# Attention outputs on one Trainium2 core: the probabilities as the stationary operand, the value tile as the moving one

## The reference

```python
def _branch_attention(q, k_cat, v_cat, slopes, window, dilation):
    ...
    m = jnp.max(sc, axis=-1, keepdims=True)
    p = jnp.exp(sc - m)
    den = jnp.sum(p, axis=-1, keepdims=True)
    o = jnp.einsum("bnrhqk,bnkrhe->bnqrhe", p / den, v_cat.astype(jnp.float32))
```

## Time and profile before

| | |
|---|---|
| median of 3 runs | 2321.32 us |
| lowest and highest run | 2320.58 and 2321.41 us |
| span of the profiled execution, first to last instruction | 2320.7 us |
| TensorE busy, of the span | 2254.3 us |
| attention in that execution | about 1086.5 to 1592 us |

### The profile page before, as it was taken

How to read it: one execution, slowest core, us unless ns; L and a number is a source line. 1 busy time by engine, 2 the same in 40 slices (tenths; PEclk the granted TensorE clock), 3 DMA queues, 4 the chain that set the end, 5 groups by cost and what they waited for, 6 DMA issues and landing times.

```text
span 2320.7 us, 32020 instructions
## 1 busy us (share of the span) xinstructions
PE 2254.3 (97%) x10792; PEld 1886.7 (81%) x10792; DVE 1509.0 (65%) x2236; ACT 940.1 (41%) x1712; POOL 477.8 (21%) x415
## 2 busy tenths in 40 slices
PE   7999997999999999999999999999799999999997
PEld 6888786888888888877888888888688888888886
DVE  5333347766666667697666666675876666666778
ACT  4111135322223234464655655565533323223443
POOL 1000014423332201053000000001543333310113
PEclk9999998999999999999999999999899999999999
DMA  5111122333333377736333323343233333337764
GB/s 146 46 55 45 51 94 64 96 99 108 104 108 106 108 263 249 252 108 173 75 69 77 77 69 73 73 114 114 73 95 104 110 105 109 101 111 260 249 224 168
DMA packets 244853, 273.98 MB, mean 118 GB/s; under 512 B 18400, under 2 KB 157664, under 8 KB 242656
## 3 DMA queue, kind: packets, MB, share of 16 engines
q1 hardware_dynamic: 241504, 260.64, 37.0%
q10 hardware_dynamic: 3200, 11.54, 1.5%
HBM read 198.20 MB, written 48.76 MB: 106 GB/s over the span
## 4 chain that ended last, share of the span: by engine, by line
PE 90%; DVE 4%; issue 2%; POOL 1%; ACT 1%; DMA 1%; DVEq 0%; SPq 0%; POOLq 0%; ACTq 0%
PE banks L1089 36%; PE banks L1136 15%; PE banks L883 11%; PE banks L1181 9%; PE banks L1012 7%; PE banks L1218 3%; PE banks L1233 3%; PE banks L1247 3%; PE banks L1261 1%; PE banks L931 1%; PE banks L1337 1%; DVE down_split L2212 1%; POOL xb_low L2731 1%; DMA raw_second<-in_o_w 0%; DVE x_lo L1933 0%
## 5 line engine op out<-in xcount | busy, mean ns | idle before, releaser
L1089 PE MATMUL banks<-xb_mid,up_split 128*128 128x512 f32 x2112 | 499.8, 392 | 4.7 <-DVE t_tile L1981 4.7
L1089 PEld LDWEIGHTS banks<-xb_mid,up_split 128*128 128x128 f32 x2112 | 400.5, 190 | 89.0 <-issue 5.5
L1136 PE MATMUL banks<-down_split 128*128 128x512 f32 x1848 | 423.0, 390 | 5.0 <-DVE down_split L2212 4.1
L1136 PEld LDWEIGHTS banks<-down_split 128*128 128x128 f32 x1848 | 345.6, 188 | 80.7 <-DVE down_split L2212 9.2
L1089 PE MATMUL banks<-xb_low,up_split 128*128 128x512 f32 x1584 | 373.5, 389 | 0.0
L1089 PEld LDWEIGHTS banks<-xb_low,up_split 128*128 128x128 f32 x1584 | 297.2, 188 | 62.2 <-issue 0.6
L2212 DVE TENSOR_TENSOR down_split<-down_raw,down_split 128x1024 fp32r<-128x1024 f32 x154 | 198.1, 1286 | 99.8 <-ACT down_split L1644 99.5
L1644 ACT CAST down_split<-down_raw 128x1024 fp32r<-128x1024 f32 x154 | 162.1, 1053 | 208.4 <-PE banks L1136 170.2
L2055 DVE TENSOR_TENSOR up_split<-sums,up_split 128x512 fp32r<-128x512 f32 x176 | 157.7, 897 | 130.0 <-ACT up_split L1499 129.7
L883 PE MATMUL banks<-x_hi,w_first 128*128 128x512 f32 x768 | 184.5, 392 | 1.2 <-ACT x_hi L1418 1.1
L2805 POOL TENSOR_TENSOR sums<-raw_up 128x512 f32<-128x512 f32 x88 | 119.6, 1361 | 320.3 <-DVE up_split L2055 162.2
(11 more groups left out here) (180 smaller groups left out, 3312.0 us busy)
## 6 DMA issues: line engine op xcount, KB each, us to landing
raw_up<-in_ffn_in_w SPq DMA_DIRECT2D x88, 512.0 KB, 5.1
down_raw<-in_ffn_out_w SPq DMA_DIRECT2D x154, 256.0 KB, 3.4
down_raw<-hid_spill SPq DMA_DIRECT2D x154, 256.0 KB, 4.0
hid_spill<-hid_mix SPq DMA_DIRECT2D x110, 256.0 KB, 2.4
down_second<-in_ffn_out_w SPq DMA_DIRECT2D x66, 256.0 KB, 3.2
k_stack<-k_parts SPq DMA_DIRECT2D x32, 512.0 KB, 6.2
raw_first<-in_conv_in_w SPq DMA_DIRECT2D x24, 512.0 KB, 3.7
hid_spill<-hid SPq DMA_DIRECT2D x44, 256.0 KB, 2.4
```

The source lines that it names most:

```text
L1089: mm = pe.matmul(bank(b_out), up_split[:, p, a, q * P:(q + 1) * P], block(RIGHT_OF[p], b)[:, q, :], start=(i == 0), stop=(i == len(passes) ...
L1136: mm = pe.matmul(bank(b_out), side[:, a, 0, i * P:(i + 1) * P], side[:, b, 1, :], start=(p in (M3, M5, M1, M2) and first and j == 0), stop ...
```

## The change

The operands of the output matmul change places. The transposed probabilities are now stationary, high part and low part in turn, and the value tile moves, 128 columns. A key tile takes two matmuls of 128 columns with a stationary operand each, all added up in one bank: 128 queries by 128 columns (64 features by the high values, 64 by the low values). The result is already queries by features. `o_second`, `o_sum`, `fold` and `turn_part` go. ScalarE scales columns 64 to 127 into `resid` (`scaled`), one pipeline step after the outputs, and VectorE then scales columns 0 to 63 and adds them to it there (`halves_added`). `o_done`, now VectorE's, frees the bank `OUT`; `o_scaled` is ScalarE's new signal. ScalarE's wait for `spilled` stands ahead of the first steps.

```diff
 # TensorE
-                    pe.wait_ge(*sum_done.at("attn", steps + s))
+                    pe.wait_ge(*o_done.at("attn", steps + s))
                     for j in range(i + 1):
-
-                        mm = pe.matmul(psum[:, OUT, 0:2 * P].rearrange("p (n q) -> p n q", n=2),
-                                       att["v_split"][pair % 2][:, j, e, :],
-                                       att["pt"][:, s % 2, :, j * P:(j + 1) * P],
-                                       start=(j == 0), stop=(j == i))
+                        for n in range(2):
+                            mm = pe.matmul(psum[:, OUT, 0:P], att["pt"][:, s % 2, n, j * P:(j + 1) * P],
+                                           att["v_split"][pair % 2][:, j, e, :],
+                                           start=(j == 0 and n == 0), stop=(j == i and n == 1))
                     mm.then_inc(pv_done.sem, 1)
-
-                def turn_part(s):
-
-                    pe.wait_ge(*sum_done.at("attn", steps + (s + 1)))
-
-                    pe.wait_ge(*o_done.at("attn", steps + s))
-                    if last and s + 1 in range(LEADS - HT, LEADS):
-                        pe.wait_ge(*lead_lo.at("attn", s + 2))
-
-                    pe.matmul(psum[:, TURN, 0:HD], att["o_sum"][:], att["fold"][:], start=True, stop=True) \
-                        .then_inc(o_turned.sem, 1)
...
                     scores(s + 1)
-                    if s >= 2:
-                        turn_part(s - 2)
                     turn_probs(s)
 # ScalarE
-                def second_part(s):
+                def scaled(s):
 
                     act.wait_ge(*pv_done.at("attn", steps + (s + 1)))
-
-                    act.wait_ge(*sum_done.at("attn", steps + s))
-                    act.copy(att["o_second"][:], psum[:, OUT, P:2 * P]).then_inc(second_done.sem, 1)
-
-                def divide(s):
-
-                    act.wait_ge(*o_turned.at("attn", steps + (s + 1)))
                     act.wait_ge(*rden_done.at("attn", steps + (s + 1)))
                     over, e, i = place(s, last)
                     pair = fixed + over
                     act.activation(resid[:, i, bass.ds(moving * P + (pair * P + e * HD), HD)],
-                                   psum[:, TURN, 0:HD], ACT.Copy, scale=rden[:, s % 2:s % 2 + 1]) \
-                        .then_inc(o_done.sem, 1)
+                                   psum[:, OUT, HD:P], ACT.Copy, scale=rden[:, s % 2:s % 2 + 1]) \
+                        .then_inc(o_scaled.sem, 1)
...
-                    if s >= 2:
-                        divide(s - 2)
                     probs_high(s)
                     if s >= 1:
-                        second_part(s - 1)
+                        scaled(s - 1)
                     exponentials(steps, s + 1)
...
+            act.wait_ge(spilled, 16)
             attend((0, 0), 0, 2, STEPS)
-            act.wait_ge(spilled, 16)
 # VectorE
-                def sum_parts(s):
-
-                    dve.wait_ge(*second_done.at("attn", steps + (s + 1)))
-
-                    dve.wait_ge(*o_turned.at("attn", steps + s))
-                    dve.tensor_tensor(att["o_sum"][:], psum[:, OUT, 0:P], att["o_second"][:],
-                                      ALU.add).then_inc(sum_done.sem, 1)
+                def halves_added(s):
+
+                    dve.wait_ge(*o_scaled.at("attn", steps + (s + 1)))
+                    over, e, i = place(s, last)
+                    pair = fixed + over
+                    o_tile = resid[:, i, bass.ds(moving * P + (pair * P + e * HD), HD)]
+                    dve.scalar_tensor_tensor(out=o_tile, in0=psum[:, OUT, 0:HD],
+                                             scalar=rden[:, s % 2:s % 2 + 1], in1=o_tile,
+                                             op0=ALU.mult, op1=ALU.add).then_inc(o_done.sem, 1)
...
                     probs_low(s)
                     if s >= 1:
-                        sum_parts(s - 1)
+                        halves_added(s - 1)
                     invert(s)
 # GpSimd
-            pool.wait_ge(*xn_ready.at("norm2", HT))
-            pool.tensor_tensor(att["fold"][:], ident[:, 0:HD], ident[:, HD:P], ALU.add) \
-                .then_inc(dist_ready.sem, 1)
```

More of the change, by code:

```diff
@@ L258, in trunk @@
                "neg_log": at(204, "neg_log", [SEQ]), "bias": at(208, "bias", [SEQ]),
-               "dist": at(212, "dist", [SEQ], F16), "v_t": at(214, "v_t", [HALF]),
-               "o_second": at(216, "o_second", [P]), "o_sum": at(216.5, "o_sum", [P]),
-               "fold": at(217, "fold", [HD])}
+               "dist": at(212, "dist", [SEQ], F16), "v_t": at(214, "v_t", [HALF])}
         dist_i = at(8, "dist_i", [SEQ], I32)
@@ L371, in trunk @@
         ph_done = signal("ph_done", attn=STEPS * PAIRS)
-        second_done = signal("second_done", attn=STEPS * PAIRS)
-        o_done = signal("o_done", attn=STEPS * PAIRS)
+        o_scaled = signal("o_scaled", attn=STEPS * PAIRS)
         lo_ready = signal("lo_ready", **chunks)
@@ L414, in trunk @@
         pl_done = signal("pl_done", attn=STEPS * PAIRS)
-        sum_done = signal("sum_done", attn=STEPS * PAIRS)
+        o_done = signal("o_done", attn=STEPS * PAIRS)
         rden_done = signal("rden_done", attn=STEPS * PAIRS)
@@ L419, in trunk @@
         gain_step = signal("gain_step", norm2=4)
-        dist_ready = signal("dist_ready", attn=2)
+        dist_ready = signal("dist_ready", attn=1)
         c12_sum = signal("c12_sum", **of_down(HT))
@@ L871, in _ @@
             grant(pe, lead_turned, half_done, chunk_done, tok_done, down_done, down_tile, up_done, xt_turned, v_turned, s_done, p_turned,
-                  pv_done, o_turned)
+                  pv_done)
             def weights(n, ph, moving=0):
@@ L1375, in _ @@
                   xn_first, xr_done, t3_hi_done,
-                  tc_hi_done, lead_hi, k_hi_done, q_hi_done, v_done, vv_hi, exp_done, ph_done, second_done,
-                  o_done)
+                  tc_hi_done, lead_hi, k_hi_done, q_hi_done, v_done, vv_hi, exp_done, ph_done,
+                  o_scaled)
             def prepare(n, moving=0):
@@ L1841, in attend @@
                             prepare(chunk0["oproj"] + LAST_CHUNK_AT[s])
-                    divide(STEPS - 2)
-                    second_part(STEPS - 1)
-                    divide(STEPS - 1)
+                    scaled(STEPS - 1)
                     prepare(chunk0["oproj"] + KT - 1)
@@ L1912, in _ @@
                   xl_ready, table_step, bias_ready, slope_ready,
-                  lead_lo, k_lo_done, q_lo_done, vv_lo, max_done, pl_done, sum_done,
+                  lead_lo, k_lo_done, q_lo_done, vv_lo, max_done, pl_done, o_done,
                   rden_done)
@@ L2566, in attend @@
                     prepare(chunk0["oproj"] + HT + 2)
-                    sum_parts(STEPS - 1)
+                    halves_added(STEPS - 1)
                     prepare(chunk0["oproj"] + KT - 1)
```

5 lines of the change are left out of this document (removed).

## The result

| | before | after |
|---|---|---|
| median, runs | 2320.97 us, 4 | 2357.53 us, 4 |
| lowest and highest run | 2320.58, 2321.41 | 2355.74, 2357.96 |
| span of the profiled execution | 2320.7 | 2355.5 |

What follows compares the result with a forecast made beforehand. TensorE was taken to bound attention; 58.2 - 6.4 - 23.4 - 1.4 = +27.0 us on a span of 2320.7, with the median 0.6 above, gave 2348 us, 1.2% slower; range 2335 to 2362, its own range 2344 to 2357.

Steps and rivals of the forecast that it cites:

- What bounds the kernel: Attention, about 1086.5 to 1592 us: TensorE busy 500.4 of 505.5 us, so changes to its stream move the end equally.
- The outputs: Output matmuls in attention: 110 ns a matmul, 220 a key tile instead of 119, over 576 key tiles: +58.2 us.
- The edge of each group: Where outputs pass to the projection, each of 128 steps wins about 0.05 us: -6.4 us, bounds nothing and 6.4.
- The fold: Removing 128 fold matmuls from TensorE: 0.17 us in 96 steps, 0.22 in 32: -23.4 us.
- Waits: TensorE's waits for the sum at the fold: a third of 4.2 us won, -1.4 us, between 0 and -4.2.
- ScalarE and VectorE: In attention, ScalarE loses 34.7 us of copies, VectorE 9 us less 4.4 added; covered by TensorE, costed at nothing.
- Nothing new is late: VectorE's wait for ScalarE, 11.4 us, stands in the same place on an engine doing less; no added delay.
- The anchor: Start of the sum: span 2320.7 us; the runs' median stands 0.6 above it, giving 2348 us.
- Loads keep ahead of the short matmuls: Rival, 8%: in output rows a key tile costs 170 ns, total about 2320 to 2326 us.
- Loads do not count: Rival, 4%: at 120 ns a key tile only the fold's loss is left, -24 to -31 us, 2290 to 2297.
- The short matmul costs more: Rival, 10%: short fp32r output matmuls cost 119 ns or above, 10.4 us more: 2358, or 2366 without edges or waits.
- VectorE's new wait reaches TensorE: Rival, 3%: ScalarE's scaling holds the output bank, each step's outputs wait 0.2 us, 26 us on top: 2374.

Runs made afterwards that it cites:

- the kernel cut in two: Kernel before, each key tile's 256-column output matmul split into two of 128 columns, each loading the same value tile again: 2377.13 us, ratio 1.024.
- the run with fewer columns: Changed kernel, but the output matmul on the low part of the probabilities moves only the 64 columns of high values: 2356.67 us, ratio to before 1.0151.
- the two banks: Changed kernel with the outputs going to two banks in turn, in all pairs but the last: 2357.33 us.
- the turned sum: Kernel before, its fold replaced by one transpose of the whole sum, then the change's ending (ScalarE scales, VectorE adds): 2328.15 us, ratio 1.0029.

## Why the prediction came out as it did

**What bounds the kernel** was right: the difference lies in attention, and TensorE is busy for 99% of it before and after. So the sum can be closed on TensorE alone, counted start to start between the two instructions of the section on the result:

| part | forecast, us | counted, us |
|---|---|---|
| outputs and the edge behind them | 58.2 - 6.4 = 51.8 | 59.0 |
| fold | -23.4 | -21.1 |
| waits for the sum | -1.4 | -3.2 |
| all else | 0 | +1.0 |
| sum | +27.0 | +35.7 |

The count gives the fold and its waits together, -24.3; they are parted by the kernel cut in two, which has the fold and almost no wait there. Of the 8.7 us that the forecast is short, 7.2 are in the first line.

**The outputs** were right in kind and nearly in size. The step took 110 ns a load from the transposes and from one pair of scores; the rows of the outputs show 110 to 112. Without the edge, the 59.0 us stand against 58.2. The kernel cut in two confirms it by itself, with 59.7.

**The edge of each group, -6.4 us, is the step that failed.** It took the distance from the first projection load to its matmul, 0.11 us before and 0.06 behind short matmuls, for a gain. The first matmul does start earlier, but the second does not. In the changed kernel its load row starts at 1320.27 (above), the first matmul at 1320.33, the second here:

```profile
1320.61 0.63 PE L1177 MATMUL banks<-x_hi,w_second 128*128 128x512 f32 x2
```

so 0.28 us after the first. In the kernel before the loads start at 1304.28 and the first matmul at 1304.39, the second here:

```profile
1304.63 0.62 PE L1181 MATMUL banks<-x_hi,w_second 128*128 128x512 f32 x2
```

so 0.24 us after it. Counted from the load it is 0.34 us after and 0.35 before: the early start is taken back one matmul later. Over the 111 rows of outputs that a projection follows, the medians say the same: the first matmul starts 58 ns sooner behind its load, the second 52 ns later behind the first. What is left is 0.7 us, so the bound that the prediction named for this term, nothing, was nearly the value. A start time next to a change of kind is no measure of pace; the sum has to run to a point where both kernels do the same.

**The fold** was sized at 23.4 us and is worth about 21. The 0.22 us for the steps with a short row of scores came from one step, behind 640 keys; behind 128 keys it is 0.17, and the usual step is 0.16 to 0.17.

**Waits** were put at -1.4 us, between 0 and -4.2, and came to -3.2. The prediction held that most of them would be met again at the next instruction; most were not, since TensorE, with longer rows of outputs, comes later to everything that it waits for. Fold and waits together were right within half a microsecond, 24.8 against 24.3, by two errors that cancel.

**ScalarE and VectorE** under cover: right that they don't count. The sizes were off: ScalarE's busy time fell by 21.5 us (940.1 to 918.6), not 34.7, VectorE's by 0.4, not 9 less 4.4. The last section has the rows. "Nothing new is late" was too strong for VectorE, whose wait for ScalarE rose from 11.4 to 28.6 us, and right for TensorE, which never waited for it.

**The anchor.** The sum started from a span of 2320.7 and added 0.6 to reach the median. In the runs of both kernels that have both figures, the time lies 1.7 us or more above the span, mostly 1.8. If that held for the profiled execution too, it took about 2322.5, over its kernel's median; its time is not on record. This and the late wait for `down_split` would explain why the difference is 36.6 us between medians, 34.8 between spans and 35.7 in attention.

**The range.** 2357.53 lies within 2335 to 2362, but half a microsecond above the forecast's own range of 2344 to 2357. The reach up to 2362 was there for a dearer matmul, which did not come; what filled it was the edge. To that extent the range held by luck. The prediction's sum without the edge would have been 2354.

**The rivals.** "Loads keep ahead of the short matmuls" fell: in the rows of outputs of the changed kernel no load starts less than 108 ns after the one before it, and the run with fewer columns has the same spacing. The Trainium skill gives about 81 ns in "TensorE: Matmul & The Clock Gate", section "Back-to-back issue gap"; for this type of operand the rows show 110 to 112, and the measurement decides. The pair of scores that spoke for the rival was no measure of a row: the load behind it came 110 ns later. "Loads do not count" fell by the same runs. "The short matmul costs more" had the right direction, but 112 is 2 ns above 110, not 9. "VectorE's new wait reaches TensorE" fell for this change by the two banks, and came true in the turned sum, where the multiply-add stood behind work that its own waiter had to release.

## What to carry to other kernels

Count stationary loads, not only columns. In this kernel, rows of fp32r matmuls with a 128x128 tile of their own came at 110 to 112 ns a load with 128 moving columns, or with 128 and 64 in turn, and at up to 119 with 256. So from 256 columns down, moving less gave 7 ns at most, and swapping operands pays only if the number of loads falls. Single starts say less: 13 of the 1024 distances between matmuls inside the changed kernel's rows are under 100 ns, the shortest 57, while no two loads there start under 108 apart. Read the pace from load start to load start over a whole row, and carry a sum on to a point where both versions do the same work; a single early start at a border may be taken back at the next instruction. When an operation is added to another engine's queue, look at what it then stands behind: if that is work which the waiter itself releases late, a short operation costs microseconds.

## What the runs showed of the hardware

A load of 64 columns in place of 128 brought the spacing in the outputs of a seven-tile step from 111 to 64 ns at the same 128 moving columns.

VectorE's multiply-add of 64 columns with one operand in the output bank took 276 ns, hardly less than the plain sum of 128 columns (282); the estimate from the slope between 128 and 512 columns had been 210. Its register instruction took 57 ns, where ScalarE's took 46:

```profile
L2508 DVEq FUSED_REGOPS  x96: 57/57/82, 1097.0 to 1495.8; - x96
```

ScalarE's copies counted 34.7 us by themselves, but its busy time fell by 21.5 only. In the records of the kernel before, 21.0 of the 34.7 us overlap the instructions beside them, and busy time counts an overlap once: the sum of such short instructions overstates what the engine gets back.
